# Second block's mixer reordered: index heads first, one round loop for attention, projections and the first recurrent tile, copies moved to ScalarE

## The chip, the cores and the metric

The kernel runs on one core of a Trainium2 chip. The metric is the time of one execution on the device in microseconds; lower is better. Times of single instructions come from one profiled execution.

## The reference

Input is 512 tokens of width 1024 in float32. Two layers of a first block run, then two layers of a second block. Only the mixer of the second block is touched:

```python
p = rms_norm(x, mix_norm[l]) @ w_in[l]                # 512 x 3280
pa, pb, pc = split_cols(p, GROUP_SPLITS)
ya = dsa_attention(pa, ...)                           # 8 heads, 2 key heads, 8 index heads
yb, v_first = rwkv7_time_mix(pb, ...)                 # 4 heads, token shift, then recurrence
yc = gated_deltanet(pc, ...)                          # 4 heads, causal conv, then recurrence
x = x + concatenate([ya, yb, yc]) @ w_out[l]

# dsa_attention, per block of 128 queries
q = rope(rms_norm(q)); k = rope(rms_norm(k)); qi = rope(qi); ki = rope(ki)
score = einsum('bqhs,bqh->bqs', relu(einsum('bqhd,bsd->bqhs', qi, ki)), wi)
_, idx = lax.top_k(where(causal, score, -inf), 128)
o = softmax(q . k[idx] * scale) @ v[idx]
```

The token shift of `yb` is `hb + (prev - hb) * mu`. The convolution of `yc` has four taps. Both recurrences are computed in chunks of 64 tokens, with a triangular system solved for each chunk.

## The kernel before

The program has one list of instructions for each engine (TensorE, VectorE, ScalarE, GpSimd, SyncE), written by functions of the same names in parallel: what TensorE does in `pick` is met by a `pick` of VectorE and one of ScalarE. Lists run in order; engines wait for each other by semaphores on named results. Where several tasks are interleaved, each is a generator, and a helper function advances them in the same order on each engine.

Weights come in tiles of at most 1024 columns per partition. SyncE loads them, ScalarE makes the high half (`wh`, line 2108), GpSimd the low half (`wl`, line 2609), and TensorE multiplies three times (high by high, high by low, low by high): lines 655 to 657 where the result has tokens in partitions, 599 to 601 where it has features in partitions (`proj_F`, 24 matmuls of 512 columns).

Mixer of the second block, `block2`, before:

- Projections with tokens in partitions: queries (512 columns), keys and values (256), index queries (512), index key and weights (72), gates of the third part (264). Results go to `pa` and `gz` by copies that ScalarE and VectorE share.
- VectorE normalizes and rotates queries and keys (lines 1999 to 2012), then rotates index queries and keys (2023 to 2024). TensorE transposes all (1239 to 1249), the other two copy. Barrier `k`.
- `dsa_rounds` (line 281): rounds in which up to four softmax units are alive, one step of the selection `pick` is done, and, in each sixth round, one of 13 projections with features in partitions (`project`). A unit is one head and one block of 128 queries: scores (701), mask added and maximum (1468, 1469), exponential (2221), transpose (709), copy (2231), product with the values (718), scaling (1493). The blocks come in the order 0, 3, 2, 1. `pick` takes, for one block, eight index scores (954), relu (2378) and weighted sum (1720, 1723), and then 16 times the eight largest (1731) and their replacement (1732); the mask is made of what was replaced (1735, 1736). It takes blocks 3, 2, 1. VectorE's `project` does the token shift (1751 to 1753) or the convolution (1760 to 1765) on the copied result.
- Barriers `l` and `m`: small loads, then the gates (2036 to 2048 and 2557 to 2568), barrier `n`.
- `tile_rounds`: the recurrence in four tiles of 128 tokens. A tile is made (lines 983 to 1110 on TensorE), then solved in five levels: product (1118), mask and copy (VectorE, 1926), two products (1130, 1137), subtraction (VectorE, 1931 and 1935); then the state is carried on (1149 to 1220) and the result normalized (1964 to 1983). The making of tile j+1 goes beside the solving of tile j.
- Barrier `o`, then the output projection.

Of the kernel before, what the change touches and what calls it, by code (L numbers as in the profile page):

```python
# [8 lines left out]
F32 = mybir.dt.float32  # L9
FR = mybir.dt.float32r  # L10
# [4 lines left out]
P = 128  # L15
# [88 lines left out]
def weight_order(A):  # L104
# [87 lines left out]
class Lane:  # L192


    def __init__(self, name, e, book):
# [17 lines left out]
        if name == "dve":  # L213
# [4 lines left out]
            self.match_replace = e.match_replace if e is not None else nothing  # L218

# [83 lines left out]
def tile_rounds(tiles):  # L303

    while not until(tiles[0], True):
        pass
    for j in range(4):
        solved, made, step = False, j == 3, 0
        while not (solved and made):
# [5 lines left out]
            if not made and (solved or step > 2):  # L315
                made = until(tiles[j + 1], True)
    for _ in tiles[3]:
        pass


def build_program(nc, A, out, dbg):
    ctx = ExitStack()
    with ctx:
# [125 lines left out]
        pa = cut(0, 5408, "p (t n) -> p t n", t=4)  # L449
# [9 lines left out]
        rr2 = cut(12320, 64, "p (t n) -> p t n", t=4)  # L459
# [4 lines left out]
        lora = cut(6656, 256)  # L464
        vdn = cut(6912, 64, "p (k n) -> p k n", k=2)
        vup = cut(6976, 256)
        gate = cut(7232, 64, "p (a t h) -> p a t h", a=4, t=4)
        ga, gb_, gg, gt = (gate[:, a] for a in range(4))
        vz = cut(7296, 512)
        UNs = [cut(7808 + 512 * n, 512) for n in range(2)]  # L470
        Ms = [cut(8832 + 256 * n, 256) for n in range(4)]
        extra = [cut(9856 + 512 * n, 512) for n in range(4)]
# [4 lines left out]
        ind = con[:, C_IND:C_IND + 2]  # L477
        vf3 = vfirst[:, :].rearrange("p (t n) -> p t n", t=4)
# [24 lines left out]
        UNITS3 = [("dsa", h, i) for i in (0, 3, 2, 1) for h in range(8)]  # L503
# [37 lines left out]
        class Stock:  # L541


            def __init__(self):
                self.free = [(spare[:, i * 512:(i + 1) * 512], None) for i in range(16)]
                self.free += [(x, None) for x in extra] + [(s[:, :], None) for s in scr]
                self.free += [(x[:, a:a + 512], None) for x in prm[1:] + wraw for a in (0, 512)]
                self.n = 0

            def get(self):  # L550
                return self.free.pop(0)

            def put(self, lane, l, *bufs):
# [3 lines left out]
                self.free += [(b, (l, self.n)) for b in bufs]  # L557

        def tensor_program(pe):
# [134 lines left out]
            def softmax(l, u, qk, vs, wide, *ready):  # L694
                nk, nb = width(u), width(u) // P
                b, free = bank(("qk", l, u), ("sm", "add" if masked(u) else "exp", l, u))
# [243 lines left out]
            def unit3(l, u):  # L940
# [3 lines left out]
                if i == 0:  # L944
                    qk.append((0, P, ident, cmask))
                return softmax(l, u, qk, [vv[:, j, g * 64:g * 64 + 64] for j in range(i + 1)], False)

            def pick(l, masks):
                for i in (3, 2, 1):
                    nk = (i + 1) * P  # L950
                    for h in range(8):
                        b, free = bank(("ix", l, i, h), ("pk", "relu", l, i, h))
                        pe.wait_ge(*free)
                        mm(b[:, 0:nk], qiT[hb(h), h // 2, i * P:nk], kid[hb(h), 0:nk], True,  # L954
# [11 lines left out]

            def rec_tile(l, j, stock):
                js = slice(j * P, (j + 1) * P)
# [7 lines left out]
                RK, VV, QK = (stock.get()[0] for _ in range(3))  # L976
# [8 lines left out]
                LW, UA = stock.get()[0], stock.get()[0]  # L985
# [6 lines left out]
                if l:  # L992
# [1891 lines left out]
```

## Time and profile before

| | us |
|---|---|
| median of 3 runs | 4472.14 (4468.44 to 4474.78) |
| the profiled execution | 4470.38 |
| its span | 4468.6 |
| TensorE matmul busy | 4039.5 (90%) |
| VectorE busy | 1619.4 (36%) |
| ScalarE busy | 1337.8 (30%) |
| GpSimd busy | 1340.4 (30%) |
| mean granted TensorE clock | 0.912 of full |

How to read it: the profile is of one execution. Busy time of TensorE includes time at the lower of its two clock levels (0.50 of full). The share over the whole span averages stages with different limits: the feed-forward parts, where TensorE runs without a gap, and the mixers, of which this case is about one. The mean of the span therefore says little of the stage that the change touches.

### The profile page before, as it was taken

To read this page: it belongs to the slowest core of one execution; us is meant where nothing else is said; L and a number is where in the kernel's file an instruction comes from. 1 tells how busy PE (TensorE), PEld (TensorE's weight loads), DVE (VectorE), ACT (ScalarE), POOL (GpSimd) and SP (SyncE) were. 2 spreads that over 40 slices of the span, in tenths; PEclk is the share of its full clock that TensorE was granted. 3 is DMA by queue.
4 is the path that set the end of the run, shared out by engine and by line. 5 is a ranking of instruction groups with operands and counts; after the bars stand their busy time and mean duration, and the time that the engine had idled before them with its cause. 6 is when DMAs were issued, how large, how long until landed. Compare 5 with 4: busy or idle time off the path is not lost.

```text
span 4468.6 us, 49638 instructions
## 1 busy us (share of the span) xinstructions
PE 4039.5 (90%) x20532; PEld 3347.4 (75%) x20532; DVE 1619.4 (36%) x3356; ACT 1337.8 (30%) x2163; POOL 1340.4 (30%) x641
## 2 busy tenths in 40 slices
PE   8988999988999799988868899989999786888999
PEld 7766887876788688875657788878888564777887
DVE  2344112245211311145767621121114576773111
ACT  2443222344322322223232132232223323113222
POOL 3104444211444444331100034434443110003443
PEclk9988999998999899987778799999999786888999
DMA  4102332201233333321000022333332100002232
GB/s 112 43 25 65 94 99 84 79 24 40 79 98 89 99 95 97 94 69 29 24 2 1 15 85 90 99 91 102 92 95 77 35 29 2 1 1 80 92 97 90
DMA packets 406704, 292.33 MB, mean 65 GB/s; under 512 B 17968, under 2 KB 356816, under 8 KB 406480
## 3 DMA queue, kind: packets, MB, share of 16 engines
q1 hardware_dynamic: 400912, 284.96, 21.3%
q10 hardware_dynamic: 5136, 2.96, 0.3%
q8 instruction: 162, 2.65, 0.3%
q0 software_dynamic: 432, 1.25, 0.1%
q14 instruction: 62, 0.51, 0.0%
HBM read 287.03 MB, written 2.10 MB: 65 GB/s over the span
## 4 chain that ended last, share of the span: by engine, by line
PE 50%; DVE 11%; ACT 3%; issue 1%; POOL 0%; ACTq 0%; DMA 0%; DVEq 0%; SPq 0%
PE ps L599 8%; PE ps L600 8%; PE ps L601 8%; PE ps L655 5%; PE ps L657 5%; PE ps L656 5%; PE ps L1130 2%; DVE arena L1732 1%; DVE cols L1731 1%; PE ps L701 1%; PE ps L718 1%; PE ps L1137 1%; PE ps L1118 1%; PE ps L954 1%; DVE mix L1360 1%
## 5 line engine op out<-in xcount | busy, mean ns | idle before, releaser
L2609 POOL TENSOR_TENSOR wl<-wraw,wh 128x1024 fp32r<-128x1024 f32 (+3 forms) x534 | 1249.1, 2340 | 2605.9 <-ACT wh L2108 2605.9
L599 PE MATMUL ps<-x_T,wh 128*128 128x512 f32 (+1 forms) x2672 | 1038.7, 389 | 33.6 <-DVE x_T L1325 23.6
L600 PE MATMUL ps<-x_T,wh 128*128 128x512 f32 (+1 forms) x2672 | 1030.8, 386 | 0.0
L601 PE MATMUL ps<-x_T,wl 128*128 128x512 f32 (+1 forms) x2672 | 1029.8, 385 | 0.0
L2108 ACT ACTIVATE wh<-wraw 128x1024 fp32r<-128x1024 f32 (+3 forms) x534 | 548.2, 1028 | 1151.9 <-PE ps L657 650.1
L599 PEld LDWEIGHTS ps<-x_T,wh 128*128 128x128 f32 x2672 | 517.6, 194 | 140.4 <-issue 39.8
L600 PEld LDWEIGHTS ps<-x_T,wh 128*128 128x128 f32 x2672 | 517.6, 194 | 95.3 <-issue 0.5
L601 PEld LDWEIGHTS ps<-x_T,wl 128*128 128x128 f32 x2672 | 516.1, 193 | 97.3
L655 PE MATMUL ps<-wh,h_T 128*128 128x512 f32 x1056 | 417.6, 395 | 27.4 <-issue 27.4
L656 PE MATMUL ps<-wl,h_T 128*128 128x512 f32 x1056 | 415.6, 394 | 0.0
L657 PE MATMUL ps<-wh,h_T 128*128 128x512 f32 x1056 | 415.5, 393 | 0.0
L1433 DVE TENSOR_TENSOR scr<-scr,ps 128x512 f32<-128x512 f32 x132 | 90.8, 688 | 662.2 <-ACT scr L2208 662.2
L2210 ACT ACTIVATE h_T<-scr 128x512 fp32r<-128x512 f32 x132 | 83.4, 632 | 591.9 <-DVE scr L1435 591.9
L655 PEld LDWEIGHTS ps<-wh,h_T 128*128 128x128 f32 x1056 | 200.6, 190 | 73.5 <-issue 32.1
L1435 DVE TENSOR_TENSOR scr<-scr,ps 128x512 f32<-128x512 f32 x132 | 90.8, 688 | 401.5 <-PE ps L601 401.3
L657 PEld LDWEIGHTS ps<-wh,h_T 128*128 128x128 f32 x1056 | 201.1, 190 | 42.4
L656 PEld LDWEIGHTS ps<-wl,h_T 128*128 128x128 f32 x1056 | 201.3, 191 | 41.8
L1458 DVE SCALAR_TENSOR_TENSOR x_tm<-ps,x_tm 128x512 f32<-128x512 f32 x64 | 40.7, 683 | 385.7 <-PE ps L657 385.7
L655 PE MATMUL ps<-wh,x_T 128*128 128x512 f32 (+3 forms) x448 | 162.1, 362 | 1.9 <-POOL wl L2609 1.9
L657 PE MATMUL ps<-wh,x_T 128*128 128x512 f32 (+3 forms) x448 | 160.9, 359 | 0.0
L656 PE MATMUL ps<-wl,x_T 128*128 128x512 f32 (+3 forms) x448 | 160.7, 359 | 0.0
L709 PE MATMUL ps<-cr,scr 128*128 128x128 f32 x376 | 83.7, 324 | 83.3 <-ACT scr L2221 80.6
(781 smaller groups left out, 5350.4 us busy)
## 6 DMA issues: line engine op xcount, KB each, us to landing
wraw<-in_ffn_w_gate_dram SPq DMA_DIRECT2D x88, 512.0 KB, 3.9
wraw<-in_ffn_w_up_dram SPq DMA_DIRECT2D x88, 512.0 KB, 3.8
wraw<-in_w_in_dram SPq DMA_DIRECT2D x82, 512.0 KB, 3.8
wraw<-in_ffn_w_down_dram SPq DMA_DIRECT2D x80, 512.0 KB, 3.6
wraw<-in_w_gate_dram SPq DMA_DIRECT2D x44, 512.0 KB, 3.9
wraw<-in_w_up_dram SPq DMA_DIRECT2D x44, 512.0 KB, 3.8
wraw<-in_w_down_dram SPq DMA_DIRECT2D x40, 512.0 KB, 3.6
wraw<-in_w_o_dram SPq DMA_DIRECT2D x16, 512.0 KB, 3.3
```

Of the source, the lines that this page charges most:

```text
L599: mm(b[:, t0:t1], wh[:, k, :], xTh[:, k, t0:t1], k == 0, False)
L600: mm(b[:, t0:t1], wh[:, k, :], xTl[:, k, t0:t1], False, False)
L601: ins = mm(b[:, t0:t1], wl[:, k, :], xTh[:, k, t0:t1], False, k == 7)
L655: mm(o, lh[:, k, t], wh[:, q, :], k == 0, False)
L656: mm(o, lh[:, k, t], wl[:, q, :], False, False)
L657: ins = mm(o, ll[:, k, t], wh[:, q, :], False, k == K - 1)
L709: ins = tr(b[:, j * P:(j + 1) * P], p_of(u)[:, j * P:(j + 1) * P])
L1130: ins = mm(b[:, hs], Dt_[:, hs], y_[:, hs], True, True)
L1433: step(tt(sg[:, :], sg[:, :], bg[:, :], ALU.mult), "ev", wg)
L1435: tt(sg[:, :], sg[:, :], bu[:, :], ALU.mult).then_inc(*v.sig("ev", wu))
L2108: copy(hl_of(w)[0], raw_of(w)).then_inc(*s.sig("w", "hi", w))
L2609: tt(wl, raw_of(w), wh.bitcast(F32), ALU.subtract).then_inc(*g.sig("w", "lo", w))
```

## The change

- The index queries are projected first, then the index key, its weights and the gates of the third part in one projection of 336 columns (before: 72 and 264), then the queries, then keys and values. ScalarE alone copies these results, into places of their own (`qitm`, `kitm`, `qtm2`, `ktm2`, `vv`, `wiv`, `gz`). The index queries and keys are rotated and transposed (`index_heads`) before the last of these projections.
- `mixer_rounds` takes the place of `dsa_rounds` and of the first part of `tile_rounds`. It first ends `heads` (normalizing, rotating and transposing queries and keys), with one `project` step in each second step. Then come the rounds: units in the order of blocks 0, 1, 2, 3, picks in the order 1, 2, 3, one `project` step in each fourth round, after that the gates, and after those at most 24 steps of the tile rounds. When all units are done, the buffers they used are given to the tiles (`over`), and the tile rounds go on. The making of tile 1 starts only then. The barriers `k`, `l`, `m` and `n` are gone.
- Masked units: one `tensor_tensor_reduce` in place of an addition and a maximum; the output's scaling goes to ScalarE.
- `project`: ScalarE copies with the first factor (1 - mu, or the last tap), VectorE adds the shifted terms straight from PSUM.
- Recurrence: three 128x512 copies of a tile, the copies of the levels (without the mask) and those of the output go from VectorE to ScalarE; the mask is applied by a predicated copy in place of the subtraction.
- Relu results go round three buffers, not two. The tile rounds' buffers (`Stock`) are a first set of 22 and a second of 15 that opens behind the attention.

The core of the diff:

```diff
-        for c0, n in ((0, 512), (512, 256), (768, 512), (1280, 72)):
-            t(w, l, 0, 8, c0, n)
-        t(w, l, 0, 8, 3016, 264)
+        t(w, l, 0, 8, 768, 512)
+        t(w, l, 0, 8, ((1280, 72), (3016, 264)), 336)
+        t(w, l, 0, 8, 0, 512)
+        t(w, l, 0, 8, 512, 256)
...
-def dsa_rounds(unit, pick, project, masks):
-
-    todo = [(h, i) for i in (0, 3, 2, 1) for h in range(8)]
-    live, n = [], 0
-    while todo or live or pick or project:
+def mixer_rounds(heads, unit, pick, project, gates, tiles, masks, stock, over):
+    n = 0
+    while next(heads, "end") != "end":
+        if n % 2 == 1:
+            next(project)
+        n += 1
+    masks.add(0)
+    todo = [(h, i) for i in range(4) for h in range(8)]
+    live, n, clear, steps = [], 0, [], 0
+    chain = tile_rounds(tiles, clear)
+    while todo or live or pick:
...
-        if project and n % 6 == 0 and next(project, "end") == "end":
-            project = None
+        if project:
+            if n % 4 == 0 and next(project, "end") == "end":
+                project = None
+        elif gates:
+            if next(gates, "end") == "end":
+                gates = None
+        elif steps < 24:
+            next(chain)
+            steps += 1
         n += 1
+    for todo in (project, gates):
+        for _ in todo or ():
+            pass
+    over()
+    clear.append(True)
+    for _ in chain:
+        pass
...
-            if not made and (solved or step > 2):
+            if not made and clear and (solved or step > 2):
                 made = until(tiles[j + 1], True)
+            yield
...
+                    v.tensor_tensor_reduce(out=p_of(u)[:, 0:nk], in0=b[:, 0:nk], in1=msk[:, i - 1, 0:nk], scale=-1.0,
+                                           scalar=3e38, op0=ALU.add, op1=ALU.min,
+                                           accum_out=m[:, 0:1]).then_inc(*v.sig("sm", "max", l, u))
...
-                    tt(rb[:, 1:512], x[:, 0:511], x[:, 1:512], ALU.subtract)
-                    step(ts(rb[:, 0:1], x[:, 0:1], -1.0, None, ALU.mult))
-                    stt(x, rb[:, :], mu[:, s:s + 1], x, ALU.mult, ALU.add).then_inc(*v.sig("pj", l, s))
+                    v.wait_ge(*at("pj", "first", l, s))
+                    stt(x[:, 1:512], psum_of("F", w)[:, 0:511], mu[:, s:s + 1], x[:, 1:512],
+                        ALU.mult, ALU.add).then_inc(*v.sig("ev", w))
...
-                        v.wait_ge(*at(*K("y", k, g)))
-                        tt(v4(ys[g]), v4(psum_of(*K("y", k, g))[:, :]), lvm(k, 0), ALU.mult).then_inc(*S("Y", k, g))
                     yield
...
-                        tt(D_, D_, psum_of(*K("d", k, g))[:, :], ALU.subtract).then_inc(*S("D", k, g))
+                        v.copy_predicated(v4(D_), lvm(k, 0).bitcast(I32), v4(psum_of(*K("d", k, g))[:, :])).then_inc(
+                            *S("D", k, g))
...
+                        ys.append(get())
+                        s.wait_ge(*at(*K("y", k, g)))
+                        copy(ys[g], psum_of(*K("y", k, g))[:, :]).then_inc(*S("Y", k, g))
```

## Rows read from the trace of the kernel before

**Rows 1.** Windows, layer 0's mixer by stages: us, busy by engine, clock, DMA share, GB/s
```profile
1910.90:1997.00 86.10, 86.02 (x482) 77.75 (x480) 36.70 (x64) 20.64 (x35) 30.69 (x14) 0.90 0.28 77
1997.00:2019.50 22.50, 7.78 (x43) 7.46 (x43) 13.46 (x34) 6.56 (x12) 0.63 (x1) 0.70 0.09 24
2019.50:2236.00 216.50, 183.53 (x678) 127.76 (x678) 141.44 (x348) 65.87 (x147) 31.89 (x13) 0.77 0.10 27
2236.00:2251.00 15.00, 1.02 (x5) 1.05 (x6) 6.91 (x17) 11.40 (x18) 0.00 (x0) 0.50 0.03 9
2251.00:2361.00 110.00, 83.09 (x603) 70.62 (x602) 78.12 (x173) 24.77 (x44) 10.06 (x12) 0.78 0.00 1
2361.00:2563.00 202.00, 170.42 (x1386) 150.93 (x1385) 139.90 (x300) 33.23 (x59) 9.57 (x12) 0.83 0.01 1
```
**Rows 2.** Windows, the scoring rounds of layer 0 by kind of work (engines: PE, PEld, DVE, ACT, POOL)
```profile
2019.50:2053.50 34.00, 31.47 (x117) 19.51 (x117) 13.81 (x36) 14.34 (x38) 4.99 (x2) 0.92 0.12 31
2053.50:2081.00 27.50, 20.74 (x82) 16.02 (x82) 26.47 (x58) 4.97 (x7) 7.17 (x3) 0.87 0.22 58
2081.00:2128.50 47.50, 41.16 (x141) 26.69 (x142) 24.30 (x52) 16.86 (x34) 2.52 (x2) 0.64 0.04 11
2128.50:2153.50 25.00, 20.54 (x85) 16.25 (x84) 22.95 (x58) 4.08 (x6) 7.10 (x3) 0.90 0.22 64
2153.50:2188.00 34.50, 30.87 (x115) 21.35 (x116) 20.23 (x50) 13.60 (x34) 2.94 (x1) 0.70 0.09 31
2188.00:2213.00 25.00, 19.40 (x82) 15.60 (x82) 22.30 (x61) 4.38 (x6) 7.16 (x3) 0.91 0.00 0
2213.00:2236.00 23.00, 19.35 (x60) 12.34 (x60) 11.39 (x37) 7.65 (x24) 0.00 (x0) 0.50 0.00 1
```
**Rows 3.** Timeline of ScalarE: first copies behind each projection
```profile
1946.40 0.66 ACT L2144 ACTIVATE arena<-ps 128x256 f32<-128x256 f32 x2 [4.64 <-PE ps L657]
...
1968.18 1.08 ACT L2144 ACTIVATE arena<-ps 128x512 f32<-128x512 f32 x2 [4.51 <-PE ps L657]
...
1984.06 0.35 ACT L2144 ACTIVATE arena<-ps 128x72 f32<-128x72 f32 x2 [14.04 <-PE ps L657]
...
1996.96 0.67 ACT L2144 ACTIVATE arena<-ps 128x264 f32<-128x264 f32 x2 [1.78 <-PE ps L657]
```
**Rows 4.** Groups of VectorE by form, rounds of layer 0: busy us, mean ns
```profile
L1731 DVE MAX8 cols<-arena 128x8 f32<-128x512 f32 x16 | 11.1, 692 | 0.4
...
L1731 DVE MAX8 cols<-arena 128x8 f32<-128x384 f32 x16 | 8.9, 558 | 0.4
```
**Rows 5.** Timelines of VectorE and GpSimd, both around 1953 us
```profile
1953.32 2.77 DVE L2009 TENSOR_TENSOR arena<-arena,pbuf 128x512 f32<-128x512 f32 x1
...
1952.80 6.98 POOL L2609 TENSOR_TENSOR wl<-wraw,wh 128x1024 fp32r<-128x1024 f32 x3 [8.57 <-ACT wh L2108]
```
**Rows 6.** Timeline of TensorE: scores of units and of the index
```profile
2092.07 2.07 PE L701 MATMUL ps<-arena,mix 64*128 64x512 f32 x2
...
2098.10 2.07 PE L701 MATMUL ps<-arena,mix 64*128 64x512 f32 x2
2099.97 1.49 PE L954 MATMUL ps<-arena 64*128 64x384 f32 x2
...
2178.34 0.91 PE L701 MATMUL ps<-arena,mix 64*128 64x384 f32 x2
...
2181.12 0.91 PE L701 MATMUL ps<-arena,mix 64*128 64x384 f32 x2
```
**Rows 7.** Groups, tiles of layer 0: a level's masked copy; a copy by ScalarE
```profile
L1926 DVE TENSOR_TENSOR spare<-ps,cr 128x512 f32<-128x512 f32 x15 | 10.2, 687 | 2.0 <-PE ps L1118 1.8
...
L2408 ACT ACTIVATE spare<-ps 128x512 f32<-128x512 f32 x4 | 2.4, 597 | 6.9 <-PE ps L983 6.9
```
**Rows 8.** Waits of TensorE in one tile, 2369.4 to 2440.5: total us, times, longest
```profile
PE ps L1118 <- DVE spare L1931: 3.9, 2, 3.7
PE ps L1190 <- DVE arena L1947: 3.5, 2, 2.8
```

More of the change, by code:

```diff
@@ L9 @@
 F32 = mybir.dt.float32
+I32 = mybir.dt.int32
 FR = mybir.dt.float32r
@@ L695, in softmax @@
                 nk, nb = width(u), width(u) // P
-                b, free = bank(("qk", l, u), ("sm", "add" if masked(u) else "exp", l, u))
+                b, free = bank(("qk", l, u), ("sm", "max" if masked(u) else "exp", l, u))
                 pe.wait_ge(*free)
@@ L1263, in block2, with over @@
-                barrier("n", l)
-                stock = Stock()
-                tile_rounds([rec_tile(l, j, stock) for j in range(4)])
+                proj_T(8, 336, xTh, xTl)
+                proj_T(8, 512, xTh, xTl)
+                index_heads(l)
+                proj_T(8, 256, xTh, xTl)
+                masks, stock = set(), Stock(l)
+                def over():
+                    pe.mark("dsa over", l)
+                    stock.open()
+                mixer_rounds(heads(l), lambda h, i: unit3(l, ("dsa", h, i)), pick(l, masks), project(), gates(l),
+                             [rec_tile(l, j, stock) for j in range(4)], masks, stock, over)
@@ L1544, in rope @@
                 tt(x1, a, b_, ALU.subtract)
-                step(tt(x2, c_, d_, ALU.add))
+                step(tt(x2, c_, d_, ALU.add), *key)
             def rope_q(l):
@@ L2043, in block2, with over @@
                 tt(gt, gt, ga, ALU.max).then_inc(*v.sig("rec", "gabs", l))
-                v.wait_ge(*at("rec", "gln", l))
-                step(stt(gt, ga, 0.0, gt, ALU.max, ALU.add))
-                v.wait_ge(*at("rec", "al", l))
-                step(tt(gg, gt, bc(sml(53)[:, 0:4].unsqueeze(1), [P, 4, 4]), ALU.mult))
-                step(ts(gg, gg, -1.0, None, ALU.mult))
-                barrier("n", l)
-                for u_ in UNs:
-                    v.memset(u_, 0.0)
-                v.memset(Ms[0], 0.0).then_inc(*v.sig("rec", "M0", l))
-                v.wait_ge(*v.own())
-                stock = Stock()
-                tile_rounds([rec_tile(l, j, stock) for j in range(4)])
+                masks, stock = set(), Stock(l)
+                def over():
+                    v.mark("dsa over", l)
+                    stock.open()
+                    for q in ENG:
+                        v.wait_ge(*at("dsa over", l, q))
+                    for u_ in UNs:
+                        v.memset(u_, 0.0)
+                    v.memset(Ms[0], 0.0).then_inc(*v.sig("rec", "M0", l))
+                    v.wait_ge(*v.own())
+                mixer_rounds(heads(l), lambda h, i: unit3(l, ("dsa", h, i)), pick(l, masks), project(l), gates(l),
+                             [rec_tile(l, j, stock) for j in range(4)], masks, stock, over)
                 barrier("o", l)
@@ new lines, in block2, with over @@
+                evac_T(8, 512, qtm2, mine=range(NT))
+                index_heads(l)
+                w = use(tiles_of(8, 256))
+                for j in range(NT):
+                    s.wait_ge(*at("w", "used", w))
+                    b = psum_of("Tm", w, j)
+                    copy(ktm2[:, j, :], b[:, 0:128])
+                    copy(vv[:, j, :], b[:, 128:256]).then_inc(*s.sig("ev", w, j))
+                masks, stock = set(), Stock(l)
+                def over():
+                    s.mark("dsa over", l)
+                    stock.open()
@@ L2575, in block2 @@
+                mixer_rounds(heads(l), lambda h, i: unit3(l, ("dsa", h, i)), pick(l, masks), project(l), gates(l),
+                             [rec_tile(l, j, stock) for j in range(4)], masks, stock, over)
                 barrier("o", l)
@@ L2636, in get @@
                 def get():
-                    buf, was = stock.get()
-                    if was:
-                        for q in ENG:
-                            g.wait_ge(*at("put", *was, q))
+                    buf, keys = stock.get()
+                    for k in keys:
+                        g.wait_ge(*at(*k))
                     return buf
```

566 lines of the change are left out of this document (332 added, 234 removed).

## Prediction

> **What bounds the kernel now.** I read the stage table first [rows 1]: the second block's mixer of layer 0 runs from 1910.9 to 2563.0 us, and its six stages are the first projections, the heads' rotation and transposes, the scoring rounds, the gates, tile 0 of the recurrence up to the point where tile 1 is made, and the rest of the tiles. The same stages fill 3385 to 4037 us in layer 1 with nearly the same lengths, so I work out layer 0 and double it. Outside the mixer the change touches nothing. TensorE is full only in the first stage. In the second and the fourth it stands almost still (7.8 of 22.5 us, 1.0 of 15.0), and in the rounds and tiles TensorE and VectorE are each busy 65 to 85% of the time in turn: a chain over several engines bounds these stages, not one engine.
>
> Second, the rounds cut at each change of what they do [rows 2]: 34.0 us of eight narrow units with 512-wide index scores; then three times a selection (27.5, 25.0, 25.0) followed by eight softmax units (47.5, 34.5, 23.0). In the selections VectorE is the bound (26.5 of 27.5). In the units TensorE is, at a low clock (0.64, 0.70, 0.50).
>
> **Part by part, layer 0, times from the start of the first projection.**
>
> *First projections.* The 72-wide projection ran 15.9 us (1968.2 to 1984.1) and the 264-wide one 12.9 [rows 3]. They are joined into one of 336 columns. Between 12.9 for 264 and 21.8 for 512 (1946.4 to 1968.2), 336 columns come to 15.5 on a straight line. 28.8 goes, 15.5 comes: 13 us off. The index transposes (20, about 4 us by the present 7.8 for 40) are put in before the last projection; the rotation they need starts behind the first projection and has 36 us of TensorE work as cover. The stage ends at 86 - 13 + 4 = 77.
>
> *Heads.* VectorE now does, behind the last projection: the sums of squares (3.4), the root (1.3), the keys (3.9), four query tiles (3.9 each, two operations of 512 columns at 0.69 and six of 256 at 0.42, on the line through 0.69 for 512 and 0.56 for 384 [rows 4]): 24 us, and its part of three interleaved projections, 2. Beside GpSimd's splitting of weights (three operations in 6.98 us) a product of 512 columns took 2.77 us, where 0.69 is the rule [rows 4, 5]: 2.1 more. Some five operations of GpSimd lie alongside, and not each is met in full: 9. Rotation ends at 77 + 5 + 35 = 117. TensorE meanwhile does four projections (22 us, 5.45 each), stands from 99 to 117, then transposes, and ScalarE copies: the first scores come at 124. Before, they came at 108.6 [rows 1], without the four projections. So picking does not begin earlier on the clock: in the code every lane ends the heads before the first pick.
>
> *Rounds.* The order by rounds follows from the code: units of block 0 in rounds 0 to 7, a selection in 8 to 24, units of block 1 in 25 to 32, selection to 49, units of block 2 to 57, selection to 74, units of block 3 to the end; the nine projections left in every fourth round to 32, gates in 37 to 43, 24 steps of tile 0 in 44 to 67. Seven terms:
> 1. Rounds 0 to 7: as the present 34.0 with its two projections, but index scores 256 wide. At 384 columns these took 1.49 us at the low clock [rows 6], so 256 columns fewer save up to 1.0 each there and half at the high one; eight times some 0.75: 28.
> 2. Selection of 256 with five projections instead of three: TensorE 5 x 5.45 = 27, VectorE 16 x 1.0 and its part of five projections, three operations of 0.75 each, 10 (now five to six operations): 28. Present one, with three: 25.0.
> 3. Units of 256, index scores of 384, two projections: the present 23.0 of such units at 0.50 is about 12 at full clock, index scores 8 x 0.75, projections 11: 29, taken as 30.
> 4. Selection of 384: 16 x (0.56 for the max [rows 4] and as much again for the replacement, 0.1 between) = 19.5, gates 8 products of 0.69, 6, and six steps of tile 0, of which VectorE works some 9 and waits for ScalarE and TensorE in the rest: 41.
> 5. Units of 384, index scores of 512, eight steps of tile 0. At the low clock a unit and its index scores repeat every 6.03 us at 512 + 384 columns [rows 6]; the same number of columns here. Eight of them 48 less the tails; at full clock a 384 unit with 256 columns of index repeats in 2.78 [rows 6]. With the tile's matmuls at 8 to 16: 50, between 38 and 60.
> 6. Selection of 512: likewise 16 x (0.69 + 0.69 + 0.1) = 23.7 [rows 4], ten steps of tile 0 on VectorE: 6 to set up, 12 updates of 0.69: 38; the chain product, copy, product, update adds waits: 45.
> 7. Eight units of 512, nothing beside them. The present end, units of 256, took 23.0 at clock 0.50 [rows 2]. The 512-wide ones take 6.03 - 1.4 (no index scores) = 4.6 each at that clock: 39.
> Sum 261, against 216.5.
> What hides the gates (15.0 before) is the selection of 384; without that cover they cost their 15 again. Added waits: every lane waits in its round for a unit and then for the tile's step, and the next max stands behind that on VectorE. ScalarE takes the output scaling (32 operations) and stays under 30% busy.
>
> *Behind the rounds.* 2 us for clearing state. Now tile 0's making, its levels and tile 1's making are 33 steps in 110.0 us [rows 1], 3.3 each. 24 of tile 0's are done in the rounds; fifteen stay, since tile 1's making starts only now. They would be 50; seven of them hold one tile instead of two: 43.
>
> *The tiles that follow,* 202.0 now. Per tile ten masked copies, three full and two half ones leave VectorE at 0.69 each [rows 7] and cost ScalarE 0.60 [rows 7]: 10 of 53 us. Little of it is on the path: TensorE waited 3.9 and 3.5 us of 71 for VectorE in a tile [rows 8]. The masks' subtraction becomes a predicated copy, which the trace does not show; nearest row 0.69, other bound two passes, 1.4; I take 0.69 (one tensor and a mask in, one out). The fused add and minimum, also unseen: 0.55 to 1.1 for 384 columns, taken at 0.6. I take 8 off: 194. Bounds 0 and 20.
>
> *Sum.* 124 (to the first scores) + 261 + 2 + 43 + 194 = 624 against 652: 28 us per layer, 56 in both. The profiled execution took 4470.4 us (span 4468.6, 1.8 around it), 1.7 below the median of the runs. 4470.4 - 56 = 4414.
>
> **The rule that speaks about the clock.** In 2081 to 2128 TensorE was busy 41.2 of 47.5 us and was granted 0.64 of its clock [rows 2], and in 2213 to 2236 19.4 of 23.0 at 0.50: 1.2 GHz, though it had hardly a gap. It had been at 0.87 to 0.91 in the selections before, with projections. I therefore price units alone at the low level. The Trainium skill, "TensorE: Matmul & The Clock Gate", Part 1, says that the throttled clock is the state of an idle engine and that sustained activity releases it. By that rule alone terms 5 and 7 would run at 2.4 GHz; the first rival prices this from rows.
>
> **Rivals.**
> - *Warm units.* With projections right before term 3 and the tile's products beside term 5 the clock stays up. Term 5 then is 38 to 40, term 6 40, term 7 24 (half the matmul time): 30 us less per layer, 4354. For it: the selections with projections have 0.87 to 0.91 [rows 2]. Against: term 4 and the second half of term 6 leave TensorE nearly idle just ahead of the units.
> - *Dear new forms.* If the predicated copy and the fused reduction take two passes, VectorE gets 72 x 0.69 + 24 x 0.55 = 63 us back per layer, and about 25 of it is on the path (term 6 and the tiles): 4414 + 50 = 4464. The change would then not take work from VectorE in the tiles. Nothing in the trace speaks for it.
> - *No overlap* (the other side). Lanes run in order, so a round can cost its unit plus its tile step instead of the longer of both. Tile 0's 24 steps took some 70 us by themselves (110.0 less nine at 4.4, which are shared with tile 1); served one after the other, in rounds 44 to 67, terms 4 to 7 sum to 20 + 15 (gates) + 43 + 24 + 39 + 70 = 211 instead of 175, and the tiles behind gain nothing: +44 per layer, 16 above now, 4502. It decides from 28 us of lost overlap per layer. For it: VectorE already works 23 to 26.5 of 25 to 27.5 us in selections. Against: TensorE and ScalarE have room there.
>
> **How the numbers follow.** Forecast 0.55 (own range 4385 to 4445), warm units 0.17, dear forms 0.12, no overlap 0.16. A measurement here tells about 0.2%, 9 us, from no change: below 4463 is faster, 4463 to 4481 the same. Faster: 0.55 + 0.17 + 0.06 of dear forms = 0.78. The same: the other 0.06 of dear forms and 0.03 of no overlap, 0.09. Slower: 0.13. The range takes in the warm case and dear forms, and leaves out no overlap and the tails: 4350 to 4468.
>
> **What would show it.** Right: the projections' stage about 77 us; first scores some 15 us later than now; no stretch like 2236 to 2251; rounds 250 to 270 long with TensorE low in the selection of 384 and at 1.2 GHz in the last eight units; after the last unit some 240 us to the mixer's end. Wrong: predicated copies near 1.4 us; a clock near 1 in units; rounds over 290 us; selections with max operations spaced far over 1.5 us by waits for tile steps.

## The result and the profile after

| | before | after |
|---|---|---|
| median, us | 4472.4 (4468.4 to 4474.8) | 4503.2 (4499.2 to 4504.0) |
| ratio | | 1.0068, 95% interval 1.0050 to 1.0085 |
| span of the profiled execution, us | 4468.6 | 4502.1 |
| VectorE busy, us | 1619.4 | 1483.7 |
| ScalarE busy, us | 1337.8 | 1423.1 |
| TensorE busy, us | 4039.5 | 4059.9 |
| mean granted clock | 0.912 | 0.899 |

The change made the kernel 31 us slower. The forecast was 4414, and 4503 lies outside its range. VectorE lost 136 us of work and the time rose: VectorE's load was not the price of these stages.

The first view is again the stage table of layer 0 in windows (length, busy time of TensorE, its weight loads, VectorE, ScalarE and GpSimd with instruction counts, clock, DMA). The eleven stages are: first projections; heads; rounds 0 to 7; selection of 256; units of 256; selection of 384; units of 384; selection of 512; units of 512; from the clearing of the state to the levels of tile 1; the rest of the tiles.

```profile
1909.90:1984.80 74.90, 74.24 (x405) 65.90 (x404) 22.33 (x40) 22.43 (x40) 30.43 (x13) 0.97 0.34 92
1984.80:2028.50 43.70, 27.42 (x123) 22.79 (x122) 31.78 (x52) 15.43 (x30) 10.52 (x4) 0.82 0.21 58
...
2028.50:2062.00 33.50, 31.95 (x107) 21.88 (x107) 7.45 (x26) 13.32 (x40) 4.76 (x2) 0.75 0.12 32
2062.00:2093.70 31.70, 30.04 (x131) 23.91 (x130) 22.03 (x62) 9.88 (x17) 11.99 (x5) 0.96 0.27 83
2093.70:2139.00 45.30, 37.45 (x114) 25.02 (x114) 14.66 (x42) 13.81 (x37) 4.73 (x2) 0.66 0.00 0
2139.00:2171.00 32.00, 15.46 (x48) 9.59 (x49) 29.72 (x81) 22.83 (x42) 0.00 (x0) 0.61 0.00 1
2171.00:2223.00 52.00, 41.96 (x144) 26.89 (x142) 25.86 (x63) 16.45 (x40) 5.38 (x6) 0.60 0.00 0
2223.00:2265.00 42.00, 23.57 (x179) 22.27 (x179) 35.94 (x79) 6.69 (x14) 0.00 (x0) 0.78 0.00 1
2265.00:2304.00 39.00, 35.00 (x112) 23.22 (x113) 7.56 (x26) 12.22 (x32) 0.00 (x0) 0.50 0.00 0
2304.00:2368.00 64.00, 49.20 (x352) 43.56 (x352) 34.59 (x85) 17.37 (x33) 4.78 (x6) 0.69 0.00 1
2368.00:2576.00 208.00, 170.69 (x1380) 153.25 (x1380) 116.24 (x256) 54.63 (x100) 9.57 (x12) 0.81 0.00 1
```

The mixer now takes 666.1 us against 652.1 [rows 1]. Layer 1 lost more: from the first projection to the last update of the state it took 653.5 us where it was 633.9, layer 0 647.6 where it was 633.3. Together that is 33.9 us, and the span grew by 33.5, so the loss lies in the two mixers. Stage by stage against the forecast:

| stage | forecast | measured |
|---|---|---|
| first projections with index transposes | 77 | 74.9 |
| heads, to the first scores | 47 | 43.7 |
| 1. rounds 0 to 7 | 28 | 33.5 |
| 2. selection of 256, five projections | 28 | 31.7 |
| 3. units of 256, index scores of 384, two projections | 30 | 45.3 |
| 4. selection of 384, gates, six tile steps | 41 | 32.0 |
| 5. units of 384, eight tile steps | 50 | 52.0 |
| 6. selection of 512, ten tile steps | 45 | 42.0 |
| 7. units of 512 | 39 | 39.0 |
| behind the rounds, to the levels of tile 1 | 45 | 64.0 |
| rest of the tiles | 194 | 208.0 |

The rounds took 275.5 us for 216.5 before, although four of the thirteen projections had moved in front of them. The first projections won 11 (with the index transposes now inside), the gates' 15 were hidden, and the stage up to tile 1's levels fell from 110 to 64. The tiles behind it got 6 longer.

The unit stages 3 and 7 have TensorE busy 37.5 of 45.3 and 35.0 of 39.0 us and a clock of 0.66 and 0.50: full of instructions, at half speed. The new forms are as cheap as was taken. Groups of VectorE by form, in a tile and in the rounds (busy us, mean ns of one):

```profile
L2087 DVE COPY_PREDICATED spare<-cr,ps 128x512 f32<-128x512 int32 x10 | 7.3, 732 | 3.8 <-PE ps L1234 3.7
...
L1797 DVE CUSTOM_DVE_ANT_0 scr<-ps,arena 128x384 f32<-128x384 f32 x8 | 4.3, 541 | 0.0
```

The predicated copy takes 0.73 us where 0.69 was taken, and the fused addition and minimum 0.54 us for 384 columns. "Dear new forms" is out.

In the tile from 2368 to 2443, TensorE's waits are (total us, times, longest):

```profile
PE ps L1222 <- DVE spare L2087: 7.3, 3, 5.0
...
PE ps L1234 <- ACT wraw L2676: 1.2, 1, 1.2
```

The product that opens a level (L1222, before L1118) now waits 7.3 us for VectorE instead of 3.9 [rows 8], though VectorE does less. ScalarE's timeline (start, length) and then VectorE's show how:

```profile
2377.44 0.60 ACT L2676 ACTIVATE spare<-ps 128x512 f32<-128x512 f32 x1 [2.72 <-PE ps L1222]
2378.33 0.60 ACT L2676 ACTIVATE spare<-ps 128x512 f32<-128x512 f32 x1 [0.30 <-PE ps L1222]
2378.95 1.28 ACT L2610 ACT_TABLE_LOAD   x1
2380.24 0.42 ACT L2610 ACTIVATE spare<-spare 128x256 f32<-128x256 f32 x1
2380.56 0.40 ACT L2612 ACTIVATE spare<-spare 128x256 f32<-128x256 f32 x1
```

```profile
2380.99 0.29 DVE L1957 TENSOR_SCALAR spare<-spare 128x256 f32<-128x256 f32 x1 [3.56 <-ACT spare L2612]
...
2381.53 0.72 DVE L2087 COPY_PREDICATED spare<-cr,ps 128x512 f32<-128x512 int32 x1
```

ScalarE first makes the level's two copies (L2676) and only then loads the table and computes the sigmoids of the next tile. VectorE needs those first (3.56 us idle) and comes to the level's predicated copy after them. TensorE, busy itself, loses only 0.3 us at this place. But VectorE is now late with the rest of the next tile's work, and the next predicated copy stands behind that. There TensorE waits 5.0 us; at the same place in the kernel before it waited 3.7:

```profile
2387.64 0.73 DVE L2087 COPY_PREDICATED spare<-cr,ps 128x512 f32<-128x512 int32 x1
...
2388.43 2.08 PE L1222 MATMUL ps<-spare,scr 128*128 128x128 f32 x8 [4.96 <-DVE spare L2087]
...
2379.82 2.05 PE L1118 MATMUL ps<-spare 128*128 128x128 f32 x8 [3.67 <-DVE spare L1931]
```

Before, VectorE did the level's copy itself and ScalarE was ahead with the next tile.

### The profile page after: what moved, and what is told of

Same layout as the page of the kernel before. It is cut to its first block, busy times and chain, and to the rows that moved or that the text cites. A ratio compares the mean times of both kernels' runs of the same rounds, so it can differ in the third digit from the quotient of the medians.

```text
span 4502.1 us, 49158 instructions
## 1 busy us (share of the span) xinstructions
PE 4059.9 (90%) x20324; PEld 3359.9 (75%) x20324; DVE 1483.7 (33%) x3096; ACT 1423.1 (32%) x2379; POOL 1338.9 (30%) x639
## 4 chain that ended last, share of the span: by engine, by line
PE 52%; DVE 10%; ACT 3%; issue 1%; POOL 0%; ACTq 0%; DMA 0%; DVEq 0%; SPq 0%
PE ps L645 8%; PE ps L646 8%; PE ps L647 8%; PE ps L701 5%; PE ps L703 5%; PE ps L702 5%; PE ps L1222 2%; PE ps L747 1%; PE ps L764 1%; DVE arena L1828 1%; PE ps L1234 1%; DVE cols L1827 1%; PE ps L1003 1%; PE ps L1241 1%; PE ps L755 1%
## 5 line engine op out<-in xcount | busy, mean ns | idle before, releaser
L2788 POOL TENSOR_TENSOR wl<-wraw,wh 128x1024 fp32r<-128x1024 f32 (+2 forms) x532 | 1247.3, 2345 | 2463.3 <-ACT wh L2221 2463.3
L2221 ACT ACTIVATE wh<-wraw 128x1024 fp32r<-128x1024 f32 (+2 forms) x532 | 548.2, 1032 | 1156.0 <-PE ps L703 652.2
L764 PEld LDWEIGHTS ps<-arena,scr 128*128 128x128 f32 x592 | 104.1, 249 | 56.9 <-issue 15.5
L701 PE MATMUL ps<-wh,x_T 128*128 128x512 f32 (+2 forms) x384 | 140.9, 367 | 3.2 <-POOL wl L2788 1.9
L703 PE MATMUL ps<-wh,x_T 128*128 128x512 f32 (+2 forms) x384 | 139.6, 363 | 0.0
```

The costliest lines, as they stand in the source:

```text
L701: mm(o, lh[:, k, t], wh[:, q, :], k == 0, False)
L703: ins = mm(o, ll[:, k, t], wh[:, q, :], False, k == K - 1)
L764: ins = mm(b[:, 0:64], q_of(u)[:, j * P:(j + 1) * P], vs[j], j == 0, j == nb - 1)
L2221: copy(hl_of(w)[0], raw_of(w)).then_inc(*s.sig("w", "hi", w))
L2788: tt(wl, raw_of(w), wh.bitcast(F32), ALU.subtract).then_inc(*g.sig("w", "lo", w))
```

## The experiments

Three causes were put up. **A**: the early steps of tile 0 do not pay, because a round serves its unit, its pick and its step one after the other, and because tile 1 can only be made after the rounds. **B**: the levels' copies on ScalarE lengthen the tiles. **C**: the unit rounds are long because TensorE is granted half its clock there, and the change made more of such rounds, with the widest units last. Ratios are to the kernel before, run on the same chip, with 95% intervals; two kernels are compared by their ratios. Beside them stands, in the text, the length of layer 0's mixer in the trace from its first projection to the last update of the state: 633.3 us in the kernel before, 647.6 in the changed one (the trace's layer 1 is named where it tells more). It is the fairer number for one edit, as the mixer's first projection began anywhere from 1904.5 to 1910.9 us in these traces, with nothing changed ahead of it.

**No early steps (e1).**

```diff
-        elif steps < 24:
+        elif steps < 0:
```

> The changed kernel with no step of tile 0 inside the rounds (24 before), all else as changed. Theory A (early steps don't pay: they lengthen the rounds about as much as they save later, since every lane serves its unit, its pick and then its tile step in turn): rounds of layer 0 go from 275.5 to about 215, the stage behind them from 64 to 110, 15 us less per layer, 4473. Theory C (the rounds are long because TensorE runs at half clock, the steps themselves lie beside other work): the rounds only lose the 34 us by which the selections and the units of 384 exceed their lengths without steps, and stay at about 242; the stage behind them gains 46: 12 more per layer, 4527.

Measured: 4516.0 us, 1.0092 (1.0065 to 1.0119), 11 us more than the changed kernel; mixer 656.4. Windows from the selection of 384 to the levels of tile 1:

```profile
2135.00:2160.50 25.50, 5.09 (x14) 2.42 (x14) 24.43 (x62) 13.24 (x25) 0.00 (x0) 0.50 0.00 1
2160.50:2195.70 35.20, 33.26 (x81) 18.19 (x81) 10.28 (x34) 12.48 (x33) 0.00 (x0) 0.50 0.00 0
2195.70:2220.50 24.80, 5.70 (x19) 3.64 (x19) 23.71 (x51) 2.22 (x7) 0.00 (x0) 0.50 0.00 0
2220.50:2259.20 38.70, 35.16 (x113) 23.39 (x114) 7.15 (x26) 12.23 (x32) 0.00 (x0) 0.50 0.00 0
2259.20:2369.00 109.80, 80.81 (x590) 69.13 (x589) 66.42 (x152) 33.96 (x62) 10.05 (x12) 0.78 0.00 1
```

The steps had cost 6.5, 16.8 and 17.2 us in terms 4, 5 and 6, 40.5 together, and they save 45.8 behind the rounds (109.8 against 64.0). So A is half right: the steps are hardly hidden, 5 us of 46 up to tile 1's levels, but they do not cost more than they bring. And without them the rounds still take 235, more than before's 216.5 with four projections fewer. A is not where the loss lies.

**Levels back on VectorE (e2), and on ScalarE in the kernel before (e4).**

```diff
-                        v.copy_predicated(v4(D_), lvm(k, 0).bitcast(I32), v4(psum_of(*K("d", k, g))[:, :])).then_inc(
-                            *S("D", k, g))
+                        tt(D_, D_, psum_of(*K("d", k, g))[:, :], ALU.subtract).then_inc(*S("D", k, g))
...
+                        tt(v4(ys[g]), v4(psum_of(*K("y", k, g))[:, :]), lvm(k, 0), ALU.mult).then_inc(*S("Y", k, g))
...
-                        copy(ys[g], psum_of(*K("y", k, g))[:, :]).then_inc(*S("Y", k, g))
```

> The changed kernel with the levels' copy, mask and subtraction back on VectorE as before, all else as changed. Theory B (ScalarE takes the copies in order, behind its own work for the next tile and its table loads, so each level waits longer): the tile period falls from 74 to about 71 and the early levels too, 12 us less per layer, 4479. Rival (the periods are longer for another reason, and VectorE gets 7 us of work per tile back): tile period 74 to 77, 4503 to 4515.

Measured: 4493.7, 1.0039 (1.0026 to 1.0051), 13 us less than the changed kernel, half of what was expected; mixer 643.9. The tiles gained 6.7 us (below), but the rounds, in which ten steps of tile 0's levels lie, became 3.0 longer. The reverse was run too, the kernel before with the levels as the change has them:

> The kernel before with only the levels changed: copy without the mask on ScalarE, predicated copy in place of the subtraction. Theory B: the tile period goes from 71 to about 74, 10 to 14 us more per layer, 4495. The step of the forecast (VectorE's work leaves the path): 5 to 8 us less per layer, 4459.

Measured: 4496.6, 1.0050 (1.0032 to 1.0069), 22 us slower than before, as expected by B; mixer 642.6. In layer 1 of this trace the mixer is 22.3 us longer, of which 12.6 lie in the rounds, which the edit does not touch (229.0 us at clock 0.73, before 216.4 at 0.77); its tiles are 9.4 longer, as in layer 0. One window for each kernel, from the clearing of the state to the last update of the state in tile 3. The kernel before, and then with these levels:

```profile
2249.90:2544.20 294.30, 243.59 (x1929) 213.58 (x1930) 211.38 (x457) 57.78 (x102) 19.64 (x24) 0.83 0.00 1
```

```profile
2244.50:2548.20 303.70, 244.83 (x1929) 216.61 (x1929) 188.79 (x416) 80.58 (x142) 19.64 (x24) 0.82 0.00 1
```

The changed kernel, and then with the levels back on VectorE:

```profile
2304.10:2557.50 253.40, 209.18 (x1671) 188.03 (x1670) 144.00 (x325) 71.03 (x129) 14.35 (x18) 0.80 0.00 1
```

```profile
2307.80:2554.50 246.70, 208.25 (x1671) 185.52 (x1669) 162.45 (x356) 53.04 (x97) 14.38 (x18) 0.81 0.00 1
```

Taking 22.6 us of work from VectorE makes these tiles 9.4 us longer; giving 18.5 us back makes the changed ones 6.7 shorter. TensorE's waits account for it: in these windows the product that opens a level waited for VectorE's result of the level ahead 13.5 us before and 22.2 with these levels, 16.6 in the changed kernel and 9.7 with the levels back. B holds in both directions. The edits move the copies and bring in the predicated copy together, and the two were not run apart; the predicated copy takes 0.73 us for 0.69, 72 times per layer, which is 3 us of the 9.4 at most.

**Only the joined projection, on the kernel before (e3).**

```diff
-        for c0, n in ((0, 512), (512, 256), (768, 512), (1280, 72)):
+        for c0, n in ((0, 512), (512, 256), (768, 512)):
             t(w, l, 0, 8, c0, n)
-        t(w, l, 0, 8, 3016, 264)
+        t(w, l, 0, 8, ((1280, 72), (3016, 264)), 336)
```

> The kernel before with only the two narrow projections (72 and 264 columns) joined to one of 336, in their old place. The term of the sum: 13 to 14 us less per layer, 4445. Rival (the rotation of the queries and keys on VectorE, or the copies, end later than the projections, so that only a part is saved): 6 less per layer, 4460.

Measured: 4460.8, 0.9961 (0.9947 to 0.9975), some 17 us less by the ratio; mixer 630.4, only 3 less in layer 0, and 631.3 for 633.9 in layer 1. The profiled execution is 7.7 us shorter than that of the kernel before, and 5.5 of it lie in the mixers; the rest of the 17 shows in no trace. The number is near the rival's, but its reason is not. The projections end some 15 us earlier and the rounds begin 11.5 earlier. Then the clock takes it back. The same 20 us of the kernel before and of this one:

```profile
2019.50:2030.00 10.50, 10.50 (x34) 6.86 (x34) 0.69 (x2) 3.32 (x4) 2.37 (x1) 0.84 0.19 51
2030.00:2040.00 10.00, 9.43 (x36) 4.90 (x36) 4.63 (x15) 5.41 (x20) 0.00 (x0) 1.00 0.00 0
```

```profile
2019.50:2030.00 10.50, 10.50 (x24) 5.50 (x24) 3.43 (x11) 3.53 (x12) 0.00 (x0) 0.52 0.00 0
2030.00:2040.00 10.00, 10.00 (x21) 4.41 (x20) 2.41 (x8) 2.76 (x9) 0.00 (x0) 0.50 0.01 2
```

In these 20 us TensorE has no gap worth naming in either kernel, and in one it is granted 0.50 where the other has 0.84 and 1.00. The same stretch of work shows it in the timelines of TensorE: from the second index score to the seventh it is 12.3 us before (2028.9 to 2041.2) and 20.2 here (2017.6 to 2037.8). The mask of the first selection came at 2080.0 before and 2078.8 here: of 11.5 us, 1.2 were left at this point. The instructions and their order are the same; only the moment of their start differs.

**Work added to raise the clock (e5, e6).** A fill of matmuls that compute nothing needed, written to the bank that the real product then overwrites:

```diff
+                for _ in range(2 if u[0] == 'dsa' and u[2] > 0 else 0):
+                    mm(b[:, :], identr, cr[:, 0:512], True, True)
                 for n, (c0, c1, lhs, rhs) in enumerate(qk):
...
+                        for _ in range(1):
+                            mm(b[:, :], identr, cr[:, 0:512], True, True)
                         mm(b[:, 0:nk], qiT[hb(h), h // 2, i * P:nk], kid[hb(h), 0:nk], True,
```

> The changed kernel, with TensorE given idle work: two matmuls of 128x128 by 512 single-pass columns ahead of the scores of each unit of blocks 1 to 3 and one ahead of each index score, into the bank that the real one then overwrites: 72 per layer. Theory C (the unit rounds are long because TensorE is granted half its clock, and more activity brings it back): the fill costs 72 x 0.23, about 16 us, at full clock, and the unit stages of 45.3, 52.0 and 39.0 us fall to about 33, 42 and 27: 34 off per layer, 4435. Rival (the granted clock does not answer to this, or TensorE's clock is not what holds the units): 72 x 0.43 = 31 us more per layer, 4565.

> As the run before, with six and two such matmuls instead of two and one: 192 per layer. Theory C: 192 x 0.23 = 44 us of fill at full clock, part of it in idle time of TensorE; unit stages of about 40, 48 and 35: 13 off per layer, 4477. Rival: 192 x 0.43 = 83 us more per layer, 4669.

Measured: 4513.4, 1.0078 (1.0054 to 1.0102), with the small fill, and 4481.4, 1.0006 (0.9992 to 1.0020), with the large one: 4 us more and 28 us less than the changed kernel. Neither theory had the number for the small fill. Its interval overlaps that of the changed kernel, and its ten executions lie wide apart, from 4482.9 us at a mean clock of 0.913 to 4532.8 at 0.902. The profiled one is the slowest of them. The units of 256 with the small fill and then the three unit stages with the large one:

```profile
2095.00:2148.00 53.00, 49.08 (x139) 29.04 (x138) 14.23 (x41) 14.19 (x38) 4.74 (x2) 0.68 0.00 0
```

```profile
2098.00:2143.00 45.00, 42.65 (x177) 27.29 (x176) 14.38 (x41) 14.91 (x39) 4.79 (x2) 1.00 0.00 0
...
2176.00:2224.00 48.00, 42.93 (x207) 26.51 (x205) 24.80 (x62) 16.99 (x41) 5.10 (x6) 1.00 0.00 1
...
2266.00:2302.50 36.50, 32.80 (x150) 22.62 (x151) 7.25 (x26) 12.25 (x32) 0.00 (x0) 0.81 0.00 0
```

The small fill leaves the clock of this execution at 0.68 and costs its time. The large one brings 1.00 in the first two unit stages and 0.81 in the third: the stage of 45.3 us takes 45.0 with 17 us of fill in it, and those of 52.0 and 39.0 take 48.0 and 36.5. Two groups of TensorE in the units of 512 show that it is the speed of the real work: the product with the values (x64), with the small fill and with the large one.

```profile
L766 PE MATMUL ps<-arena,scr 128*128 128x64 f32 x64 | 15.7, 428 | 1.5 <-ACT scr L2557 1.5
```

```profile
L766 PE MATMUL ps<-arena,scr 128*128 128x64 f32 x64 | 9.7, 299 | 1.5 <-ACT scr L2557 1.5
```

C holds: 192 added matmuls a layer make the changed kernel faster. It is not linear, and it is not a matter of gaps, as TensorE was busy 49.1 of 53.0 us with the small fill. The Trainium skill, "TensorE: Matmul & The Clock Gate", Part 1, says that activity releases the throttle; the trace agrees in direction, but shows that a TensorE busy 35.0 of 39.0 us can stay at 0.50, which being busy alone would not explain.

**The widest units early (e7)**, the order of blocks as before:

```diff
-    todo = [(h, i) for i in range(4) for h in range(8)]
+    todo = [(h, i) for i in (0, 3, 2, 1) for h in range(8)]
...
-                for i in (1, 2, 3):
+                for i in (3, 2, 1):
```

> The changed kernel with the blocks' order of before: picks 3, 2, 1 and units 0, 3, 2, 1, all else as changed. If the order is what makes the rounds long (the widest units end alone at clock 0.50): the last stage is of units of 256, 23 us instead of 39, and the units of 512 lie beside the 384-wide index scores and two projections in about the 45 to 47 us that the kernel before took: 16 less per layer, 4471. Rival (the width only moves: the units of 512 take 60 where those of 256 took 45): 4503.

Measured: 4460.8, 0.9963 (0.9948 to 0.9978), 47 us less than the changed kernel; mixer 627.1. The units beside the 384-wide index scores and the last units:

```profile
2104.00:2149.50 45.50, 38.56 (x156) 26.02 (x156) 17.27 (x43) 16.95 (x38) 4.76 (x2) 0.79 0.00 1
...
2259.50:2281.60 22.10, 19.61 (x64) 12.95 (x65) 4.86 (x25) 8.82 (x32) 0.00 (x0) 0.50 0.00 0
```

Units of 512 beside those scores and two projections take 45.5, as those of 256 took 45.3: the clock is 0.79 instead of 0.66. The end falls from 39.0 to 22.1. This is the largest single effect, 22 us per layer, and the edit of the change that I did not price as such.

**Projections in selections only (e8).**

```diff
-            if n % 4 == 0 and next(project, "end") == "end":
+            if n in (8, 11, 14, 17, 20, 23, 33, 36, 39) and next(project, "end") == "end":
```

> The changed kernel with the nine projections of its rounds only in the selections (six in the first, three in the second), none in unit rounds; gates and tile steps begin three rounds later. If a projection beside units costs its own time and beside a selection nothing: the units of 256 fall from 45 to 35, the second selection grows by 3: 7 less per layer, 4489. Rival (projections also hold the clock up for the units): the units of 256 take 42 at clock 0.50, and nothing is won, 4503.

Measured: 4508.3, 1.0065 (1.0043 to 1.0087), the same as the changed kernel. The edit did more than was meant: the list of projections only ends at a tenth call, so gates and tile steps did not come into the rounds at all. Against the run without early steps, then: selection of 256 and units of 256 took

```profile
2048.70:2087.50 38.80, 35.95 (x156) 28.82 (x155) 23.48 (x63) 11.57 (x19) 14.38 (x6) 0.96 0.33 95
2087.50:2113.60 26.10, 24.31 (x64) 14.69 (x65) 8.26 (x34) 10.50 (x33) 0.00 (x0) 0.53 0.01 1
```

64.9 for 77.3 there (32.3 and 45.0), at a lower clock in the units. From the first scores to the last mask it was 182.4 for 196.1. So the placing pays, and the gates outside cost it again: of the 13.7 us, 3.2 were left in the mixer (653.2 against 656.4).

**Combinations.** e9: the order of before and the levels on VectorE. e10: also the projections in the selections (six in the first, three in the second, with the tenth call). e11: e9 with the large fill. e12: the kernel before with the joined projection and the large fill.

> The changed kernel with the two edits that helped singly: picks 3, 2, 1 and units 0, 3, 2, 1, and the levels back on VectorE. If both causes stand beside each other (42 us for the order, 9 for the levels): 4452, below both kernels. Rival (VectorE's added 7 us per tile falls on the selections, in which the tile's steps lie now): the gain of the levels goes, 4462.

> As e9, with the nine projections of the rounds in the selections only (six in the first, three in the second; the gates and the tile's steps start a few rounds later). From the run with that schedule before: units of 256 columns with index scores took 26 us instead of 45, the selections 39 and 35 instead of 32 and 25. The theory that units pay for projections and selections don't: 8 less per layer, 4436. Rival (what the units gain the selections lose, and the clock falls to 0.50 in the units): no change, 4452.

> As e9, with the fill of the larger kind (six matmuls ahead of a unit's scores, two ahead of an index score). Theory C: the clock is 1.00 in the unit stages with fill; the stages have less to win than in the order 1, 2, 3 (the last one is 22 us long): 5 less per layer than e9, 4442. Rival (the fill costs 41 us at full clock where little is left to win): 5 more per layer, 4462.

Measured: 4445.6, 0.9920 (0.9898 to 0.9943); 4432.0, **0.9896 (0.9874 to 0.9917)**; 4462.8, 0.9961 (0.9945 to 0.9977). The second beats both kernels, by 1.0% and 1.7%; the three mixers are 619.2, 616.5 and 630.0. In the trace of the second, layer 0, units of 512 and units of 384 (with tile steps):

```profile
2093.50:2132.60 39.10, 36.58 (x98) 21.93 (x99) 10.70 (x34) 12.95 (x32) 0.00 (x0) 0.50 0.00 0
...
2173.00:2208.00 35.00, 30.58 (x117) 19.35 (x117) 17.47 (x60) 21.80 (x51) 4.98 (x6) 0.71 0.00 0
```

The units of 512, without projections, take 39.1 us at clock 0.50 where it was 45.5 with two, and the units of 384 35.0 where it was 41.7 in e7. The rounds are 251.0 long against 255.7 in e9. By the ratio e10 is 11 us faster than e9, of which the mixer of layer 0 shows 2.7: its first projection began at 1904.5 us here and at 1909.7 there, and nothing ahead of it differs. Layer 1 shows more: its mixer took 616.5 us for 626.4 in e9, and its rounds, from the first scores to the last product with the values, 252.2 for 262.7. The placing gains in both layers; how much of the difference between the layers is the clock's (0.72 here and 0.71 in e9, in the rounds of layer 1) stays open.

The fill brought nothing here: over the rounds the clock rose to 0.89 from 0.73, but they took 267 us for 256, since with the short units last there is less to win and the fill itself has to be run.

> The kernel before with the joined projection and the larger fill. In the run with the joined projection alone the scores began 11.5 us earlier and the rounds then ran at clock 0.50 where before had 0.84 to 1.00, so that 4 of the 15 us were left after them. Theory C: with the clock up the 15 us stay, and the unit stages of 47.5, 34.5 and 23.0 us at 0.64, 0.70 and 0.50 lose a few more: 4440 against 4461. Rival (the fill costs what it brings): 4461.

Measured: 4467.7, 0.9981 (0.9965 to 0.9997): the same holds for the kernel before. With the fill its rounds, from the first scores to the last product with the values, ran at 0.93 and took 229 us for 225 without. The clock can be bought with this fill, but here it costs what it brings. C's number for this run was wrong by 28 us.

**What the early steps (e13) and the other copies (e14) are worth, in the better order.**

> As e10, without the 24 early steps of tile 0. In the old order they cost 41 us in the rounds and saved 46 behind them. Theory A' (they pay only a little in any order, since what overlap they win in the rounds is lost between tile 0 and the making of tile 1): 5 us more per layer than e10, 4442. Rival (in this order they lie in unit rounds, where VectorE is idle, so the rounds shrink by only 25 without them): 20 more per layer, 4472.

> As e10, with the other copies of a tile back on VectorE too: VV, F2, F3 of 512 columns and the two halves of the output. Theory B' (any copy that ScalarE takes in its order lengthens the tiles): tile period 66 to 70 in e10 falls to about 64 to 68, 6 us less per layer, 4420. The forecast's step (these 4 x 0.69 us are off VectorE's path): 3 to 8 us more per layer, 4442. Neither, if they lie beside other work: 4432.

Measured: 4456.3, 0.9954 (0.9941 to 0.9966), without early steps: 26 us slower than e10 by the ratios, between the two forecasts; mixer 625.4. Its rounds are 219.2 us and the tiles 288.0, against 251.0 and 247.3: in this order the steps cost 32 and save 41.

With all copies on VectorE 4447.4, 0.9933 (0.9920 to 0.9947). From the clearing of the state to the last update it took

```profile
2282.00:2529.60 247.60, 207.98 (x1671) 184.87 (x1670) 170.46 (x371) 46.22 (x82) 14.36 (x18) 0.82 0.00 1
```

247.6, for 247.3 in e10. So in the tiles these copies lie beside other work on either engine; B' falls, and so does the forecast's term for them there. The rounds were 3.6 us longer (254.6 for 251.0), with tile 0's copies on VectorE there; the mixer, at 620.4, is 3.9 longer in all, and that of layer 1 4.0 (620.5 for 616.5). Taking these copies off VectorE is thus worth some 4 us per layer, in the rounds and not in the tiles. Of the rest of the 16 us, 4.8 lie ahead of the first mixer, where the two programs are the same.

## Why the prediction was wrong, point by point

- **First projections and heads**: 118.6 measured for 124, the joined projection right in its place. That it would come through to the end was taken for granted: on the kernel before only some 9 of its 13 us per layer were left in the time, and in the trace 3 in either layer. In layer 0 a lower clock in the rounds behind it ate most of them (e3).
- **Term 3 failed first, 45.3 for 30.** It took half the length of units at clock 0.50, on the ground that two projections beside them would keep the clock up. The granted clock was 0.66. With the clock at 1.00 the stage took 45.0 with 17 us of fill, about 28 without it if all of the fill lay in the path (an estimate), so the 30 was right for a clock that the stage did not get. I had argued for the low level in terms 5 and 7 and not in 3. Terms 1 and 2 missed by 5.5 and 3.7 in the same direction, term 1 at 0.75 where before had 0.92 [rows 2].
- **Terms 4 to 7 sum to 165 for 175.** Term 4 was overpriced (its steps cost 6.5 us), 5 and 6 about right (52.0 and 42.0 for 50 and 45, with steps that cost 16.8 and 17.2); term 7 was right to the microsecond. But I computed what the order of blocks costs (39 at the end where before has 23) and never set it against the alternative; e7 shows that order to cost 22 us per layer.
- **Behind the rounds, 64.0 for 45: the term was mis-sized by an average.** 33 steps in 110 us gave 3.3 each. They are of two kinds: by the code, 15 steps make tile 0 and 18 solve it, with tile 1 made beside 15 of those. In the trace of the run without early steps the first product of tile 0's levels starts at 2297.4, 38.2 us behind the clearing: 2.5 for each of the 15. The other 18 take 71.6, 4.0 each. The 24 early steps were the 15 cheap ones and the start of the levels with no tile 1 beside it: 46 us saved and not 65. The 15 that stay all hold a step of tile 1's making and took 4.3 us each.
- **The tiles, 208 for 194: the sign was wrong.** The step "VectorE's work leaves the path" took a load for a chain. What left VectorE went into ScalarE's order, behind and ahead of the next tile's sigmoids, squares and table loads. Levels: 9.4 us longer in the kernel before, 6.7 in the changed one (e4, e2). The other copies: 0 within the tiles, 4 us per layer in the rounds (e14).
- **The sum.** The terms missed by -5.4 (to the first scores), +5.5, +3.7, +15.3, -9.0, +2.0, -3.0 and 0 (the rounds), +19.0 (up to tile 1's levels) and +14.0 (the tiles): 42 us, 666 for 624. Term 3, the stage behind the rounds and the sign of the tiles are the steps of the forecast that failed.
- **Rivals.** "Dear new forms" is refuted by 0.73 and 0.54 us. "Warm units" did not happen; the large fill shows its clock, and that reaching it costs about what it gives. "No overlap" named 4502, and 4503 was measured, but only half of it is what happened: the early steps are served nearly one after the other (40.5 of 45.8 us paid), as it says, while its price of 70 us for them was as wrong as its silence on the order and the levels. The number agrees by cancellation.

Per layer, then, against the kernel before: the order of blocks about 22 us and the levels 7 to 9 lost, and the joined projection, the hidden gates and the early steps won. Shown by runs are the order, the levels and the clock's part in the unit stages. What decides which clock a stretch gets is not settled here.

## What to carry to other kernels

In a stage that several engines share, find out first at which clock TensorE runs it, and try what needs TensorE under the stretches that VectorE bounds; here the widest TensorE work alone at the end cost 22 us per layer. A copy moved to an idle engine also enters that engine's order: ask what stands ahead of it and who waits for what is now behind it. And when a stage is priced by steps, price each kind of step from its own stretch, not the stage by their number.

## What the hardware showed that was not expected

TensorE can be busy 35.0 of 39.0 us with small float32 matmuls, most of 64 rows or 64 columns, and be granted 0.50 throughout. Added matmuls of 128 rows and 512 columns did nothing at two per unit (0.68 for 0.66 in the units of 256) and brought 1.00 at six, in two unit stages of three; the third, of 512, had 0.81. Ten executions of the kernel with the small fill took 4482.9 to 4532.8 us at mean clocks of 0.913 to 0.900. The same instructions, in a kernel whose rounds started 11.5 us earlier, took 20.2 us at 0.50 to 0.52 instead of 12.3 at 0.84 to 1.00. Ahead of the first mixer, where no edit touched the program, the traces differ too: the mixer began anywhere from 1904.5 to 1910.9 us. A difference of some 5 us in one trace is therefore no effect of an edit until the stages that it touches show it.
